# Unread TensorE products ahead of the wait for the normed tiles, at four of six norms

## The reference

```python
def rmsnorm(x, gain):
    x32 = x.astype(jnp.float32)
    y = x32 * lax.rsqrt(jnp.mean(x32 * x32, axis=-1, keepdims=True) + RMS_EPS)
    return (y * gain.astype(jnp.float32)).astype(x.dtype)

def second_block(...):
    h = x
    for l in range(DEPTH):
        h = h + hybrid_mixer(rmsnorm_2(h, norm_mix[l]), ...)
        h = h + peer_ffn(rmsnorm_2(h, norm_ffn[l]), ...)
    return rmsnorm_2(h, norm_final)
```

## Time and profile before

| | us |
|---|---|
| median of three runs | 1651.59 |
| lowest, highest | 1651.34, 1653.29 |
| the profiled execution, its own time | 1654.7 |
| its span, first to last instruction | 1651.8 |
| TensorE busy | 1528.0 (93%) |
| VectorE busy | 1179.7 (71%) |
| ScalarE busy | 818.8 (50%) |
| mean granted TensorE clock | 0.961 |

### The profile page before, as it was taken

How to read it: one execution, slowest core, us unless ns; L and a number is a source line. 1 busy time by engine, 2 the same in 40 slices (tenths; PEclk the granted TensorE clock), 3 DMA queues, 4 the chain that set the end, 5 groups by cost and what they waited for, 6 DMA issues and landing times.

```text
span 1651.8 us, 30049 instructions
## 1 busy us (share of the span) xinstructions
PE 1528.0 (93%) x10218; PEld 1406.4 (85%) x10218; DVE 1179.7 (71%) x2186; ACT 818.8 (50%) x1217; POOL 15.9 (1%) x16
## 2 busy tenths in 40 slices
PE   6899886999989999988999799799989999999997
PEld 5788775999869999867999798799968888889996
DVE  4676655788655645655379888799979999987665
ACT  6443555554455445545476566355533333334443
POOL 0000000000021000000000000000000000000000
PEclk9998989999989989989999999899989999999998
DMA  6443342555644432244467476344467777765553
GB/s 257 115 149 101 103 140 77 156 184 184 204 128 155 157 101 74 77 146 160 154 204 228 160 223 204 121 137 141 143 201 240 241 244 240 241 223 190 189 180 127
DMA packets 97771, 276.62 MB, mean 167 GB/s; under 512 B 10788, under 2 KB 37540, under 8 KB 97188
## 3 DMA queue, kind: packets, MB, share of 16 engines
q1 hardware_dynamic: 65808, 240.92, 45.7%
q10 hardware_dynamic: 31892, 34.75, 6.3%
HBM read 259.37 MB, written 16.25 MB: 167 GB/s over the span
## 4 chain that ended last, share of the span: by engine, by line
PE 80%; DVE 10%; ACT 5%; issue 2%; DMA 2%; ACTq 0%; DVEq 0%; SPq 0%; PEldq 0%
PE acc L1055 7%; PE acc L1058 7%; PE acc L1059 7%; PE ring L534 6%; PE ring L537 6%; PE ring L538 6%; PE acc L986 5%; PE acc L990 5%; PE acc L991 5%; PE acc L534 4%; PE ring L1021 4%; PE acc L537 3%; PE acc L538 3%; DVE sb_lo L1542 2%; PE ring L1042 2%
## 5 line engine op out<-in xcount | busy, mean ns | idle before, releaser
L1542 DVE TENSOR_TENSOR sb_lo<-sb_raw,sb_hi 128x1024 fp32r<-128x1024 f32 x450 | 546.6, 1229 | 221.6 <-ACT sb_hi L1117 204.5
L1117 ACT ACTIVATE sb_hi<-sb_raw 128x1024 fp32r<-128x1024 f32 x450 | 469.9, 1057 | 392.1 <-PE acc L1055 168.3
L986 PE MATMUL acc<-sb_XH,sb_hi 128*128 128x256 f32 x800 | 236.0, 295 | 18.2 <-DVE sb_lo L1542 13.2
L534 PE MATMUL ring<-sb_XH,sb_hi 128*128 128x256 f32 x784 | 224.4, 286 | 7.5 <-DVE sb_lo L1542 7.5
L990 PE MATMUL acc<-sb_XL,sb_hi 128*128 128x256 f32 x800 | 227.9, 285 | 0.0
L991 PE MATMUL acc<-sb_XH,sb_lo 128*128 128x256 f32 x800 | 227.8, 285 | 0.0
L537 PE MATMUL ring<-sb_XL,sb_hi 128*128 128x256 f32 x784 | 223.5, 285 | 0.0
L538 PE MATMUL ring<-sb_XH,sb_lo 128*128 128x256 f32 x784 | 223.4, 285 | 0.0
L1055 PE MATMUL acc<-sb_hi,sb_coefh 128*128 128x512 f32 x512 | 200.7, 392 | 7.6 <-DVE sb_coefl L2041 7.6
L1058 PE MATMUL acc<-sb_lo,sb_coefh 128*128 128x512 f32 x512 | 200.5, 392 | 0.0
L1059 PE MATMUL acc<-sb_hi,sb_coefl 128*128 128x512 f32 x512 | 200.1, 391 | 0.0
(11 more groups left out here) (320 smaller groups left out, 2585.9 us busy)
## 6 DMA issues: line engine op xcount, KB each, us to landing
sb_raw<-wstream SPq DMA_DIRECT2D x450, 512.0 KB, 3.6
ahead<-sb_early ACTq DMA_DIRECT2D x100, 128.0 KB, 2.2
sb_area<-ahead ACTq DMA_DIRECT2D x100, 128.0 KB, 3.2
sb_area<-gains ACTq DMA_DIRECT2D x4, 512.0 KB, 4.9
sb_area<-consts SPq DMA_DIRECT2D x1, 1782.0 KB, 16.6
sb_area<-mem ACTq DMA_DIRECT2D x1, 1024.0 KB, 11.5
relvec<-sb_area ACTq DMA_DIRECT2D x1, 1024.0 KB
sb_area<-keys ACTq DMA_DIRECT2D x1, 1024.0 KB, 4.8
```

The lines of the kernel that those rows point to most:

```text
L534: ins = mm(out, w[0], x[0], start=first, stop=False)
L986: ins = mm(o, w[0], XH[:, c, :], start=c == 0, stop=False)
L1117: A(hi[:, r, :], raw[:, r, :], ACT.Copy).then_inc(S("hi_ready"), 1)
L1542: tt(lo[:, r, :], raw[:, r, :], hi[:, r, :].bitcast(F32), ALU.subtract).then_inc(S("lo_ready"), 1)
```

## The change

A new helper `keep_awake(name, n)` takes the bank that the norm's first transposes will use and runs n products of 512 columns into it, each with `start=True, stop=True`. They read the activations `XH` and `XL` as the previous stage left them. Nobody reads their result: the transposes write over it. `norm_T` calls it ahead of its first wait at joints 2, 3 and 4 with 20 products and at joint 5 with 8. That makes 68 new products. Lines behind it in the file move by 8: L554 becomes L562, L565 becomes L573, L568 becomes L576, L573 becomes L581.

```diff
             X2 = (XH, XL)
 
+            def keep_awake(name, n):
+
+                b = bank(name)
+                for i in range(n):
+                    mm(b, XH[:, 0, 0:P], XL[:, 0:2, :].rearrange("p c t -> p (c t)"), start=True, stop=True)
+
             def norm_T(k):
 
+                if k >= 2:
+                    keep_awake(("xn", k, 0), 8 if k == 5 else 20)
                 for t in range(NT):
                     pe.wait_ge(S("xn_ready"), NT * k + t + 1)
```

## The result

| | before | after |
|---|---|---|
| median of 12 runs, us | 1652.34 | 1655.54 |
| lowest, highest | 1650.80, 1653.89 | 1651.53, 1660.12 |
| ratio after to before | | 1.0023, 95% interval 1.0015 to 1.0030 |
| the profiled execution: time, span | 1654.7, 1651.8 | 1652.27, 1650.5 |

The changed kernel is slower by 0.23%, and its times spread over 8.6 us where the kernel before spreads over 3.1. The forecast was 1650.0, range 1646.8 to 1653.4. The profiled execution of after is one of its fastest and shows none of the loss; the loss had to be looked for in further traces. Two single executions in what follows, 1921.65 us (in e3) and 2501.56 us (the kernel before, beside g1 to g4), count in no ratio.

A forecast was written before the change was run, and what follows sets the result against it. TensorE, busy 93%, was taken as the bound, its largest wait (33.5 us) being transposes waiting for VectorE's normed tile. Median 1651.59 minus 1.6 (4.6 lost before, 3.0 after) gave 1650.0 us, range 1646.8 to 1653.4.

The forecast's parts named there:

- joints: Four places, 2 to 5, where the norm's transposes on TensorE wait for VectorE's normed tile: 5.78, 5.60, 6.00, 2.48 us idle.
- the gap: TensorE's idle time ahead of a joint's first transpose; 20 products (4.54 us) or 8 (1.82) were to fit in it.
- B: From the fresh projection's first product to the first L534, 24 products: 3.09 us at full clock, 4.57 after a fall.
- A: From a joint's first transpose to the fresh projection's first product: 4.80, 4.79, 4.85, 4.40 us; 4.40 expected at full clock.
- the 0.4 of the prediction: Transposes at half clock make A 0.4 us longer; the fill was to bring it to 4.4 at joints 2 to 4.
- A + B: Both pieces over four joints: 36.17 us in the profiled execution, 29.96 at full clock, 35.88 at the lower end.
- a gain of 1.6: Expected saving over the four joints against the median: 4.6 us lost before, 3.0 after.
- one half each way: At each joint the clock's fall was given even odds of costing time, before and after; 1.48 us per fallen B after.
- the slower rival: Fall moves from the gap into B, costing 1.48; each long joint goes from 7.88 to 8.97, total 1654.9; chance 0.1.
- The gain isn't lost behind the joints: After joints 2 and 3 weights come in time, only 0.3 us of waits, and TensorE then runs nearly without gaps.
- either way: Other short half-clock stretches (scores, routing) shift against their work, by a joint's 1.5 us, faster or slower.
- the rival of the moved fall: The same as the slower rival: fall moved from the gap into B, 1654.9 us, chance 0.1.

The follow-up runs named there:

- e3: Changed kernel plus 36 unread products behind the transposes of the four joints, up to the first projection; 1652.13 us, ratio 0.9997.
- g1: Changed kernel, joints untouched, plus unread products in the waits of the cross attention behind joint 2; 1651.89 us, ratio 0.9996.
- g4: f3 plus unread products in five more waits of the second block; 1644.58 us, ratio 0.9952.
- e2: Changed kernel with its 68 products 16 columns wide in place of 512; 1652.93 us against 1652.31, ratio 1.0001.
- f1: Kernel before, no fill, with 16 unread products behind the cross attention's query projection, so the attention starts 2.9 us later; 1658.91 us, ratio 1.0039.
- g2: Kernel before with the unread products of g1 in the cross attention alone; 1650.77 us against 1652.85, ratio 0.9990.
- e1: Changed kernel run again without an edit, for a second trace; 1655.32 us, ratio 1.0016.
- f4: Changed kernel run a third time without an edit, for one more trace; 1657.09 us, ratio 1.0027.
- e4: Changed kernel with the fill at joints 2, 3 and 4 alone, none at joint 5; 1655.74 us, ratio 1.0017.
- f2: Changed kernel with 6 unread products behind the cross attention's query projection, to start the attention 0.7 us later; 1652.80 us, ratio 1.0012.
- f3: e3 plus unread products in the waits of the cross attention; 1649.61 us, ratio 0.9985.
- g3: f3 without the change's 68 products ahead of the transposes; 1650.04 us, ratio 0.9988.

## Why the prediction was wrong

The mechanism at the joints was right: the fill hides in the gap, and the clock falls later, in B or not at all. The fill takes the time forecast (4.70 us for 20 with the last one's tail, against 4.54), leaves 1.25 us at joint 2, and delays nothing. B is 3.1, or 4.2 to 4.6 with a clock of 0.64 to 0.70, and once 4.90, where the fall came early (0.55). A falls from 4.8 to 4.58 at joints 2 and 3, 0.2 and not 0.4. There ScalarE issues a DMA (L1199, 234.19 to 234.53 us at joint 2) just ahead of its row of copies, which starts at 234.58, 0.95 us behind the first transpose; before it was 1.15. No copy in the row waits. At joint 4, which has no such issue, it went from 1.21 to 0.75, and A from 4.85 to 4.38, the 0.4 of the prediction.

A + B is 0.3, 1.7 and 1.9 us less in the three traces of the changed kernel; the forecast was a gain of 1.6. That this fits is in part luck, for "one half each way" was wrong on both sides. The forecast had 34.5 us for the kernel before (29.96 at full clock and 4.6 lost) and 32.9 after (3.0 lost); measured are 36.2 to 36.3 in the four traces with the joints of the kernel before (before, e2, f1, g2), and 35.9, 34.5 and 34.3 after. Of the twelve B in the three traces of the changed kernel ten fell and two held. The forecast also started from a median of three, 1651.59; that of twelve is 0.75 higher. Joint 3 lost 1.1 to 1.4 in B, as the slower rival said, but the others outweighed it.

The step that failed is "The gain isn't lost behind the joints". I checked there only that no wait for weights would swallow the gain, and put the shift of other half-clock stretches at a joint's 1.5 us "either way" with a chance of 0.01 of a slower kernel. The runs show that the shift has a cost in one place far above that: 4.3 to 4.5 us in the cross attention behind joint 2 (e1, f4, e4), where the kernel before (traces of before and e2) is at full clock and has nothing to gain. The same three traces have 1.2 us more behind joint 4, 0.1 to 0.2 more behind joint 3 (the end of joint 3's own half-clock stretch), and 0.6 to 0.9 less in the rest. With the 1.7 and 1.9 gained in the joints this gives 1426.6 and 1426.9 from joint 2 on in e1 and f4, 3.0 and 3.3 over the kernel before; the medians differ by 3.2. The 1.2 behind joint 4 isn't one-sided: over all traces that row goes from 260.8 to 265.6, and what decides it is not shown (joint 4 kept its clock in e1 and in f2, which have 265.03 and 261.25; it fell in g1, which has 265.58).

Why is it a loss behind joint 2? The cross attention is a row of short products and waits, and its clock holds or falls according to where it lies against the clock's changes. In the kernel before, joint 2 always entered its projection at half clock in the traces that I have, and the clock rose in it, 0.4 us before its 24 products were done (rise at 243.8, first L534 at 244.2). From there the attention holds its clock: 38.5 us in before and in e2. The trace of after has the same order (rise at 242.6, first L534 at 243.1) and the same 38.5 us. Where the fill kept the clock longer, joint 2's fall is later and shorter, its projection ends 0.1 to 0.3 us before the rise (e1: rise at 241.2, first L534 at 241.1; e4 and f4 0.3), and the attention lies 0.5 to 0.8 us earlier against it. That a shift of the attention alone brings such falls, without any fill, is shown by f1, in both the place and the size. That the attention's falls are most of the loss is shown by g1, where no loss is left that can be measured (0.9996); that they are all of it is not shown, since the same products also made the kernel before faster (g2). That other executions without a trace are divided in the same way is inferred from their times.

The chances were wrong with it. I had the rival of the moved fall at 0.1, and had it look for its price in B alone; its 1654.9 lies close to the measured 1655.5 by luck, for the joints gained. The Trainium skill's sentence on transposes (TensorE: Matmul & The Clock Gate, Part 4) was no help in either direction: in after the clock stayed at 1.00 over joint 3's 16 transposes, though their 2.2 us were all that TensorE did in the 5.6 us between the fill and the projection.

## What to carry to other kernels

A fill that keeps TensorE's clock up in one gap changes where the following stretches lie against the clock's next changes. Price the stretches behind it that are full of short waits, not only the gap: there a gain of 2 us turned into a loss of 3. In this kernel the gain came only as more of the waits were filled: nothing with the four joints alone, even with a bridge to the projection (e3), 0.15% with the attention (f3), and 0.5% with five more waits (g4). And where an execution's time is far from the median, take several traces before believing one: the profiled execution of after was faster than that of before.

## What the runs showed of the hardware that was not expected

A stretch at full clock repeats almost exactly; what varies between executions is where the clock falls. Behind joint 2 it is 38.52, 38.53 and 38.52 us in before, after and e2, although the way to joint 2 varied by 0.8 us among them. Behind joint 3 it is 184.58 to 184.61 us in eight of the eleven columns, whether the joints had half-clock stretches (before, g2) or none at all (e3, f3, g4). So a rise of the clock ahead of a stretch is not needed for it to repeat, and it doesn't protect it either: e1, f4 and e4 have a rise inside dense work at joint 2, 0.1 to 0.3 us behind the first L534, and fall in the attention.

A part with no edit in it can take two times for the same reason. The kernel's first 228 us vary by 3 us over the traces (225.3 to 228.3 to the last wide product before joint 2), and most of that lies at about 135 to 167 us. From TensorE's 801st to its 1001st product five of the fourteen traces (e1, e3, g1, g2, g3) take 29.5 to 29.6 us, and the other nine 31.9 to 32.2. The half-clock stretches that begin between 120 and 170 us sum to 10.2 us in the five and to 13.7 in the nine. Why an execution takes the one or the other is not shown.
